# Prompt attention with query tiles taken alternately from the longest and the shortest

## What is computed

```python
def block(i):
    s = i * Q_BLOCK
    pos_q = s + jnp.arange(Q_BLOCK)
    ...
    return nsa_core(qb, pos_q, gb, kc, vc, pos_c, ks_blk, vs_blk, wb[:, 0], wb[:, 1], pos_w, ovl)
o = lax.map(block, jnp.arange(T // Q_BLOCK))

def nsa_core(q, pos_q, gates, kc, vc, pos_c, ks_blk, vs_blk, kw, vw, pos_w, ovl):
    p_c = masked_softmax(jnp.einsum('bgrqd,bgnd->bgrqn', q, kc), pos_c[None, :] <= pos_q[:, None])
    ...
    p_s = masked_softmax(jnp.einsum('bgrqd,bgqkd->bgrqk', q, k_sel), m_s.reshape(B, G, 1, Tq, -1))
    ...
    p_w = masked_softmax(jnp.einsum('bgrqd,bgkd->bgrqk', q, kw), m_w)
    ...
    return gates[..., 0:1] * o_c + gates[..., 1:2] * o_s + gates[..., 2:3] * o_w
```

## Time and profile before

| what | value |
|---|---|
| median of 3 runs | 2288.47 us |
| profiled execution | 2286.91 us |
| its span | 2285.1 us |
| busy in the span: PE, VectorE, ScalarE, GpSimd | 2097.3, 895.9, 521.0, 562.3 us |
| the attention stage, first to last probability transpose | 709.0 to 992.7 us |

### The profile page before, as it was taken

One profiled execution on the slowest core, in us unless ns is written; L12 is line 12 of the kernel. 1 busy time (PEld: TensorE's weight loads), 2 busy tenths in 40 slices (PEclk: granted clock), 3 DMA queues, 4 the chain that ended last, 5 costly groups with the idle time before them and its releaser, 6 DMA issues. The chain is left out here.

```text
span 2285.1 us, 46305 instructions
## 1 busy us (share of the span) xinstructions
PE 2097.3 (92%) x18884; PEld 1518.7 (66%) x18884; DVE 895.9 (39%) x2063; ACT 521.0 (23%) x1470; POOL 562.3 (25%) x643
## 2 busy tenths in 40 slices
PE   8999999899888999978987999999999999898976
PEld 6446664588775666646666888884568777667732
DVE  2015444355466766634553534332564111111111
ACT  2211111234334555533421111110111111111100
POOL 1027112122240111230023524442211222222222
PEclk9999999999989999999997999999989999999999
DMA  5001040000060000055546122114567999999997
GB/s 176 29 30 39 34 159 2 1 2 2 2 112 7 1 2 1 2 132 175 156 123 156 28 56 67 54 38 141 195 244 270 368 370 373 370 368 370 369 378 269
DMA packets 169601, 323.95 MB, mean 142 GB/s; under 512 B 34207, under 2 KB 102312, under 8 KB 169182
## 3 DMA queue, kind: packets, MB, share of 16 engines
q1 hardware_dynamic: 149270, 293.02, 36.9%
q0 software_dynamic: 12096, 21.43, 4.0%
q10 hardware_dynamic: 8016, 6.46, 0.9%
HBM read 302.03 MB, written 40.36 MB: 150 GB/s over the span
## 5 line engine op out<-in xcount | busy, mean ns | idle before, releaser
L428 PE MATMUL psum<-w,hT 128*128 128x512 f32 (+1 forms) x512 | 203.3, 555 | 0.0
L428 PE MATMUL psum<-hT,w 128*128 128x344 f32 x576 | 169.1, 454 | 0.0
L428 PEld LDWEIGHTS psum<-w,hT 128*128 128x128 f32 x512 | 97.7, 194 | 97.3 <-issue 89.8
L1654 ACT ACTIVATE a_P<-psum,a_nmax 128x512 f32<-128x512 f32 (+4 forms) x256 | 123.3, 496 | 135.5 <-DVE a_nmax L1547 85.5
L428 PEld LDWEIGHTS psum<-hT,w 128*128 128x128 f32 x576 | 108.6, 190 | 57.1 <-ACT dnT L479 0.9
L1543 DVE TENSOR_REDUCE a_nmax<-psum 128x2 f32<-128x1024 f32 (+4 forms) x128 | 90.3, 736 | 50.4 <-PE psum L1452 42.5
L2872 PE MATMUL psum<-f_wg,f_xT 128*32 128x384 f32 x864 | 97.4, 487 | 9.5 <-DMA f_wg<-w_gate 8.8
L2806 POOL DMA_INDIRECT f_x<-h_rows,tokens x36 | 37.8, 1050 | 276.5 <-PE psum L2857 168.9
L2872 PE MATMUL psum<-f_wu,f_xT 128*32 128x384 f32 x864 | 97.2, 487 | 4.9 <-DMA f_wu<-w_up 4.9
L2874 PE MATMUL psum<-f_wg,f_xT 128*32 128x128 f32 x864 | 98.5, 273 | 0.0
L2874 PE MATMUL psum<-f_wu,f_xT 128*32 128x128 f32 x864 | 98.3, 273 | 0.0
(11 more groups left out here) (631 smaller groups left out, 4470.7 us busy)
## 6 DMA issues: line engine op xcount, KB each, us to landing
f_wg<-w_gate SPq DMA_DIRECT2D x64, 1024.0 KB, 21.3
f_wu<-w_up SPq DMA_DIRECT2D x64, 1024.0 KB, 22.0
f_wd<-w_down SPq DMA_DIRECT2D x64, 1024.0 KB, 21.6
k_stage<-cache_nsa SPq DMA_DIRECT2D x128, 192.0 KB, 2.5
w<-w_in SPq DMA_DIRECT2D x6, 2048.0 KB, 8.3
x_wg<-w_in SPq DMA_DIRECT2D x16, 512.0 KB, 4.8
x<-x_prompt SPq DMA_DIRECT2D x8, 512.0 KB, 6.1
o_w<-w_out SPq DMA_DIRECT2D x2, 2048.0 KB, 8.4
```

The source lines that it names most:

```text
L428: ins = nc.tensor.matmul(PS[i % 4][0:m_rows, 0:n], lhsT, rhs, start=(k == 0), stop=(k == KD - 1))
L1654: ins = nc.scalar.activation(Pb[u % 2][:, g, o:o + w], S[n % 2][:, g, col:col + w], ACT.Exp, bias=nmax[:, u % 2, c0 + g:c0 + g + 1], accum ...
```

## The change

The list of units is built in another order: for `n` from 0 to 3, and for each of the four head pairs, tile `7 - n` and then tile `n`. Each pair of tiles is so taken four times: (7, 0), (6, 1), (5, 2), (4, 3). Nothing else is edited; the instructions of a unit are the same.

```diff
-        units = [(i, j) for i in reversed(range(NT)) for j in range(4)]
+        units = [(i, j) for n in range(NT // 2) for j in range(4) for i in (NT - 1 - n, n)]
```

## The result

The changed kernel takes **2319.93 us** (median of 4 runs, 2317.52 to 2322.22), the kernel before 2287.40 us beside it (4 runs): ratio **1.0142**, 95% interval 1.0126 to 1.0157, so 32.5 us slower. The forecast was 2305.0 us, with a range of 2297 to 2321. The sign was right, and the forecast change, 16.5 us, is about half of what came. The profiled execution took 2319.38 us, with a span of 2317.7 us.

The account below looks back on a forecast made before the run. PE's program order was taken to bound tiles 7 to 3, a VectorE, ScalarE, GpSimd chain the rest. Pairs, 78.4 + 76.6 + 77.2 + 74.0 less 2.25, sum to 303.95 against 287.59 us: +16.4, so 2305.0; range 2297 to 2321.

Parts of the forecast that it names:

- at equal PE busy time: Attention stage in the profile after: about 16 us longer, with PE's busy time unchanged.
- Stall A: Short unit: PE waits for GpSimd's spread; 2.65, 2.05, 1.75 us in tiles 0, 1, 2; some 25 us in total.
- Stall B: Following long unit: PE waits for a score buffer freed by late exponentials; 2.0, 1.8, 1.5 us in tiles 7, 6, 5.
- The 0.4 us for the bank: Long unit of tile 7: ScalarE's first-quad copy, queued behind late exponentials, holds a transpose bank about 0.4 us more.
- rival (3): Slower still: PE's granted clock falls behind the waits in the pairs, giving 2315 or 2335 us; chance 0.20.
- four pairs: Clock falling in the four pairs of tiles 7 and 0, 2.5 us each, 10 us together: 2315 us.
- all twelve: Clock falling in all twelve pairs with a Stall A over 1.7 us: 2335 us.
- It can go both ways: Earlier trace: clock 0.50 after a 2.84 us wait, 1.00 after a 2.64 us wait behind dense work.
- 4, 3: 18.5 us: Pair of tiles 4 and 3: short phase 10.15 with a 1.8 us stall, long unit 8.35; 18.5 us.
- no B: Tile 4's unit, paired with tile 3: no Stall B, as its second scores start early in the short unit.
- Rivals (1): Faster: long units fill short ones' gaps, three quarters of 17 us idle going, 2275 us; chance 0.07.
- (2): No difference: about 54 us of added stalls a third smaller would cancel all 16 us, 2288 us; chance 0.08.

Follow-up runs that it names:

- run 2: Changed kernel, with VectorE working out the scales of tiles 0 to 3 at the unit's start, ahead of the next unit's maxima: 2315.76 us, ratio 1.0142.
- Run 4: Changed kernel; in tiles 4 to 7 next unit's first scores and maxima behind the second transposes, first quad copied by VectorE, not ScalarE: 2289.02 us, ratio 1.0016.
- run 5: Changed kernel, with 8, 6, 5 unneeded products before spread transposes of tiles 0, 1, 2 and 7, 6, 5 before next scores in tiles 7, 6, 5: 2309.12 us.
- Run 8: Changed kernel; in tile 4's units, tile 3's last quads weighed ahead of the scores and its totals multiplied ahead of the maxima: 2317.86 us, ratio 1.0135.
- run 9: Changed kernel with the edits of run 2 and Run 4 together: 2283.54 us, ratio 0.9991 to the kernel before.
- run 10: Kernel before, in its own order, with only the scales of tiles 0 to 3 worked out early, as in run 2: 2279.44 us, ratio 0.9972.
- one edit alone: Changed kernel, with only the next unit's first scores moved behind the second transposes in tiles 4 to 7: 2317.21 us, ratio 1.0145.
- the other: Changed kernel, with only VectorE copying the first four transposed blocks of tiles 4 to 7: 2317.76 us, ratio 1.0146.
- run 1: Changed kernel, with 12 unneeded products ahead of the spread transposes (tiles 0 to 2) and 12 ahead of next scores (tiles 7 to 5): 2330.14 us.

## Why the prediction was right in sign and short in size

- **Where the loss is.** Right: all of it in the stage. Not right was "at equal PE busy time": 7.8 us more in the stage, which already points to the clock.
- **Stall A.** Right as a moment: the spread at 5.88 us for 5.85, and 21.5 us of waits in all for "some 25". The listed waits are shorter than the sum's (2.26, 1.73 and 1.45 for 2.65, 2.05 and 1.75), because PE arrived later (766.34 us, 3.62 into the unit for 3.2), not because the spread came earlier. That its end was due to the spread alone was not so: run 2 shows the second layer behind it.
- **Stall B.** Right: 1.97, 1.75 and 1.53 us for 2.0, 1.8 and 1.5, and 26.5 us of waits at the scores, about as much as for the spread. Run 4 shows that without it, and without tile 4's wait that went with it, almost all of the loss is gone. The 0.4 us for the bank, booked in the 7, 0 pairs alone, was about 0.2.
- **The step that failed first** is the place of rival (3): a fallen clock was weighed as another case, at 0.20, and its price left out of the sum, where it came on top of the forecast's waits. Size: 11.1 us (run 5), 1.6 of it in the stage's first unit, where the clock falls in the kernel before as well. Only wait A was held against the earlier trace rows, and only in "four pairs" or "all twelve" at 2.5 us each. The rows of after show six falls of 1.1 to 1.6 us, four behind B and two behind A, in the 7, 0 and 6, 1 pairs; and run 4, with A alone, still has two. "It can go both ways" is what the rows show; which way a given wait goes stays open.
- **The term that was mis-sized** is "4, 3: 18.5 us": the pairs took 20 (7.0 us in all). "no B" was right for scores, but L1573 was followed only in the short units, not in tile 4, where it stands behind the maxima in the same way; the earlier trace rows have no row of it, though the trace of before does. Run 8 gives 4.7 of the 7.0. About 0.5 of the other 2.3 is what run 8 left of the last B, which the sum books under the 5, 2 pairs and which falls into the first unit of tile 4; the rest was not taken apart. The 5, 2 pairs, 0.8 over their sum at full clock, were not either.
- Together: 11.1 + 7.0 + 0.8, less 0.3 by which the 7, 0 pairs came under their sum at full clock, is 18.6.
- **The range.** That 2319.93 us lies in it is in part luck. The forecast's own bounds ended at 2313, and the upper 8 us were there for rival (3); they were used up by the clock and by tile 4's missed wait together.
- **Rivals (1) and (2).** Ruled out by the run. The Trainium skill, Perfetto Trace Analysis, Optimization Strategy, says that interleaving regimes with different most-contended engines may improve performance; here the stage grew by 35.0 us, and with the waits repaired (run 9) it is still 4 us longer than the order before with the early scales alone (run 10).

## What to carry to other kernels

In software-pipelined code each step of the next unit has a fixed place inside the present one, so a unit must be long enough to cover its *successor's* chain; mixing long and short units breaks that at each handover, whatever the averages of busy time say. When a wait is summed, ask what stands right behind it for the same releaser (here one edit alone brought 1.3 us, the other 1.6, both 34.1), and follow each product that is queued behind longer work in *both* units of a pair. Where the new waits of TensorE are about as long as waits behind which its clock has been seen to fall, put the price of some falls into the forecast, with a range, and not into a case beside it: here six of sixteen such waits cost 1.1 to 1.6 us each.

## What the runs showed of the hardware

- The granted clock fell from 1.00 to 0.50 behind six of the sixteen waits of 1.68 to 2.26 us, with PE busy on both sides of them, and stayed at 1.00 behind the other ten (change). Two waits of 2.26 and 1.96 us in one pair (748.85 and 754.60) left it at 1.00, two of 2.26 and 1.97 in the next (768.60 and 774.21) did not; a wait of 2.21 us with no second one behind it lowered it too (run 4, 781.04). Behind the change's eleven waits of 1.40 to 1.53 us it stayed at 1.00.
- One such fall made the stretch from one spread to the next 1.1 to 1.6 us longer (12.43 us against 13.57, and 12.26 against 13.88).
- Eight transposes took 1.97 us in such a stretch (775.90) and 1.09 us 3 us later (778.87).
- Unneeded products in PE's idle time made the stage 11.1 us shorter (run 5); made longer than the wait by 0.4 to 1.2 us, they made the kernel slower than without them (run 1).
